# Weight slots of the last stage filled while the second mixer ends, and the first mixer's last sums stored in the second

## The chip, the core and the metric

The kernel runs on one core of one Trainium2 chip. Its time is the device time of one launch in microseconds (us), lower is better. TensorE multiplies matrices and transposes, VectorE (DVE in the rows), ScalarE (ACT) and GpSimd (POOL) work on whole tiles, and SyncE (SP) issues the transfers between the chip's main memory and the on-chip memory. Each engine has its own list of instructions and runs it in order; semaphores hold an engine until another one, or a transfer, has got far enough.

## The reference

One encoder layer on 2048 tokens of width 1024:

```python
xn = rms_norm(h, g_attn_pre)
qa, ka, va, qb, kb, vb = split(xn @ w_in)
ya = mixer_a(qa, ka, va)       # grouped attention over all tokens, 8 query heads, 2 key heads
yb = mixer_b(qb, kb, vb)       # dilated windows with a position bias, 8 heads
y = concat(rms_norm(ya, g_out_a), rms_norm(yb, g_out_b)) @ w_out
h = h + rms_norm(y, g_attn_post)
f = square(relu(rms_norm(h, g_mlp_pre) @ w_ff1)) @ w_ff2
h = h + rms_norm(f, g_mlp_post)
gate = sigmoid(rms_norm(h, g_ple) @ w_ple_gate)
h = h + gate * (p @ w_ple_proj)
```

Everything is float32. Most factors are split into a high and a low part (the names end in `_hi` and `_lo`), and a product is then three matmuls: high by high, high by low, low by high.

## The kernel before

It has four stages, each a block of its own with a program for each engine. At the end of a block all engines meet at a barrier, and what SyncE must have seen land is waited for there. The stages are `project_phase`, `mixer_a_phase`, `mixer_b_phase` and `feed_phase`; in the rows their tiles begin with `proj`, `mixa`, `mixb` and `feed`. Orders are written out by hand in each engine's function; no scheduler is at work. Tiles live in the on-chip memory, some from the left (for one stage) and some from the right (`side="right"`, kept over into the next stage).

**First mixer.** 16 query blocks of 128 rows, two groups of heads each. For each unit VectorE writes two half products into `y_half` (L1089), GpSimd adds the halves (L833) and the parts (L837) into `y_st`, and SyncE stores it (L715). The last such pair of sums, `summed(2 * NT + 1, ...)`, and its store stand at the very end of the block.

**Second mixer.** 8 heads of 16 units; even heads use the first of two sets of keys, queries and values (`kT[0]`, `qT[0]`, `v_hl[0]`), odd heads the second. The last head is odd. GpSimd splits the next head's inputs in units 0 to 7, then copies its bias tables (`other_tables`, `end_tables`), and in each unit adds two halves (L1343) that TensorE transposes back (L1438). It opens the stage with memsets and the first head's tables. SyncE loads the next head's inputs behind waits for these splits: keys (L88), queries (L93), values (L98 and 24 small ones, L106), tables (L113, L119). Before the last head it loads the constants of the next stage, and after that head's first store the rows of `total` (L145, L146).

**Last stage.** It works on blocks of 512 tokens. The first block starts with the output product: for each of four token tiles TensorE transposes (L1872) and multiplies (L1964) 24 times with the weights in four slots `w_split`, 1 MB each, then 24 times with those in `w_far`, four more pieces of 1 MB that lie in `feed_comb` for now. Later all weights go through the four slots (L1881): some are loaded as pairs from `wG`, others are loaded raw and split by ScalarE and GpSimd. SyncE's list at the start of the stage is: four slots (L1757), four residual tiles `res` (L1772), four far pieces (L1775), each waiting for its slot's landing, and four raw weights (L1778).

Of the kernel before, what the change touches and what calls it, by code (L numbers as in the profile page):

```python
# [15 lines left out]
F32 = mybir.dt.float32  # L16
F32R = mybir.dt.float32r
# [3 lines left out]
P = 128  # L21
# [47 lines left out]
class HeadInputs:  # L69
# [6 lines left out]
    def __init__(self, nc, ctx, scr):  # L76
        k = Kit(nc, ctx, "mixb")
        self.scr = scr
        self.q_in = k.sb("q_in", [P, S])
        self.k_in = k.sb("k_in", [P, S])  # L80
        self.v_in = k.sb("v_in", [P, self.VT, HD])
        self.t_near = k.sb("t_near", [P, TABLE_W - OWN_W])
        self.t_own = [k.sb(f"t_own{u}", [P, 7 * P]) for u in range(2)]
        self.k_dma, self.q_dma, self.v_dma, self.t_dma = (k.sem(n) for n in ("k_dma", "q_dma", "v_dma", "t_dma"))

# [37 lines left out]
class FeedInputs:  # L123
# [6 lines left out]
    def __init__(self, nc, ctx):  # L130
        k = Kit(nc, ctx, "feed")
        self.total = k.sb("total", [P, TT, D], side="right")
        self.g_row = k.sb("g_row", [P, 2, D], side="right")
        self.gate_in = k.sb("gate_in", [P, 3, KD], side="right")
        self.const_in = k.sem("const_in")
        self.w_dma, self.out_dma = k.sems("w_dma", self.NR4), k.sems("out_dma", TT)

    def load_consts(self, sp, gates, gains):
        for i, g in enumerate(gates):
            sp.dma_start(self.gate_in[:, i, :], g).then_inc(self.const_in, 16)  # L140
        for i, g in enumerate(gains):
            sp.dma_start(self.g_row[:, i, :], row_broadcast(g)).then_inc(self.const_in, 16)

    def load_y(self, sp, scr, t):
# [493 lines left out]
def mixer_a_phase(nc, scr, step, ident, first, heads, w_ff2, w_late):  # L638
# [12 lines left out]
    with ExitStack() as ctx:  # L651
# [8 lines left out]
        oT = k.sb("oT", [P, 2, BANK])  # L660
        y_half = k.sb("y_half", [P, 2, G * 2 * HD])
        q_raw = heads.t_own[1][:, 0:G * P]
        y_st = k.sb("y_st", [P, 2, G * HD])
        nmax = k.sb("nmax", [P, 2, 2, G])
# [23 lines left out]
        row_done, merge, scale_done = k.sem("row_done"), k.sem("merge"), k.sem("scale_done")  # L688
        o_done, fold_done, half_done, y_done = (k.sem(n) for n in ("o_done", "fold_done", "half_done", "y_done"))
        y_out = k.sems("y_out", 2)  # L690
# [16 lines left out]
        def _(sp):  # L707
# [81 lines left out]
            one(NT - 1, None)  # L789
            store(1, slice(NT * P, NT * P + P), 2 * NT + 1)  # L790
            sp.wait_ge(y_out[0], 16 * (NT + 1))
            sp.wait_ge(y_out[1], 16 * (NT + 2))
            sp.wait_ge(q_dma, 32 * NT)

        @block.gpsimd
        def _(pool):
# [101 lines left out]
            for it in range(NHB + SPLIT_ITS + 1, NT):  # L898
                for w in range(2):
                    unit(it, w)  # L900
            summed(2 * NT + 1, 1, 16 * NT + 16, 2 * NT * MERGE + 1)

# [230 lines left out]
def mixer_b_phase(nc, scr, step, ident, heads, feed, consts):  # L1133
# [13 lines left out]
    with ExitStack() as ctx:  # L1147
        k = Kit(nc, ctx, "mixb")
        q_in, k_in, v_in, t_near, t_own = heads.q_in, heads.k_in, heads.v_in, heads.t_near, heads.t_own
        kT = [[k.sb(f"kT{u}{h}", [P, SW], F32R) for h in range(2)] for u in range(2)]  # L1150
        qT = [k.sb(f"qT{u}", [P, S], F32R) for u in range(2)]
        v_hl = [k.sb(f"v_hl{u}", [P, VT, 2 * HD], F32R) for u in range(2)]
        t_oth = [k.sb(f"t_oth{u}", [P, 6, P]) for u in range(2)]
# [41 lines left out]
        def _(sp):  # L1195
# [34 lines left out]
            sp.wait_ge(pre_lo, len(FIRST_ORDER))  # L1230
            heads.load_k(sp, 1)
            sp.wait_ge(pre_lo, PRE)
            heads.load_q(sp, 1)
            next_v(0, 1)
            next_tables(0, 0, 1)
            for h in range(NHB - 1):
                one(h)
            feed.load_consts(sp, *consts)
            store(NHB - 1, 0)
            sp.wait_ge(y_out[0], 32 * NHB)  # L1240
            sp.wait_ge(y_out[1], 32 * NHB - 16)
            for t in range(TT):
                feed.load_y(sp, scr, t)
# [13 lines left out]
        def _(pool):  # L1257
# [56 lines left out]
            def split_values(h, par, m):  # L1314
# [7 lines left out]
                pool.tensor_tensor(low, v_in[:, at, :], hi.bitcast(F32), ALU.subtract).then_inc(v_lo, 1)  # L1322

            borders(0)
            pool.wait_ge(set_done, 3)
            pool.wait_ge(t_dma, 32)
            other_tables(0)
            end_tables(0, (0,))
            borders(1)
            pool.memset(o_sum[:, 1, :], 0.0).then_inc(set_done, 1)  # L1330
# [278 lines left out]
def feed_phase(nc, x, w_ff2, w_tail, pT_d, scr, out, step, ident, feed):  # L1609
# [44 lines left out]
    with ExitStack() as ctx:  # L1654
# [11 lines left out]
        w_raw = k.sb("w_raw", [P, NR4, CW])  # L1666
        w_sp = [k.sb(f"w_split{i}", [P, 2, CW], F32R) for i in range(NSPL4)]
        res = k.sb("res", [P, TT, D])
# [54 lines left out]
        def _(sp):  # L1723
# [29 lines left out]
            def load_split(C, j, slot):  # L1753

                if not (isinstance(C, int) and C < NSPL4):
                    sp.wait_ge(w_used, C - NSPL4 + 2)
                sp.dma_start(w_sp[slot][:].bitcast(F32), scr["wG"][j]).then_inc(w_dma[slot], 16)  # L1757
# [10 lines left out]

            for C in range(NSPL4):
                load_split(C, C, C)  # L1770
            for t in range(TT):
                sp.dma_start(res[:, t, :], x[t * P:(t + 1) * P, :]).then_inc(x_dma[t], 16)  # L1772
            for q in range(NR4):
                sp.wait_ge(w_dma[q], 16)
                sp.dma_start(w_far[q].bitcast(F32), scr["wG"][NR4 + q]).then_inc(w_dma[q], 16)  # L1775
            for i in range(NR4):
                sp.wait_ge(w_dma[i], 16 * (NG1 // NR4))
# [764 lines left out]
```

## Time and profile before

| | |
|---|---|
| median of 3 runs | 3391.04 us (3388.26 to 3392.82) |
| the profiled execution | 3389.53 us |
| its span | 3387.7 us |
| TensorE busy | 3301.4 us, 97% of the span |
| VectorE busy | 2298.8 us, 68% |
| ScalarE busy | 1857.0 us, 55% |
| GpSimd busy | 1856.9 us, 55% |
| transfers | 503.39 MB, mean 149 GB/s |

The span is from the first to the last instruction of one profiled execution; the time of that execution is a little longer. TensorE's share is the mean over all stages, so what matters for a change is where TensorE isn't busy, and what it waits for there. In the rows, L with a number is a line of the kernel, "SPq" is SyncE's queue of transfers, and "[2.57 <-DVE feed_xT L2266]" means that the engine sat idle for 2.57 us before this row and that VectorE's instruction of line 2266, writing `feed_xT`, ended that. A row may stand for several alike ("x24").

### The profile page before, as it was taken

The numbers are of one execution on the slowest core, as the hardware profiler recorded it, in microseconds if no ns is written. First come the engines' busy times: TensorE is split into PE (matmuls) and PEld (weight loads), VectorE is DVE, ScalarE is ACT, GpSimd is POOL, SyncE is SP. The second block draws the span as 40 slices with busy tenths as digits, with TensorE's granted clock in tenths as the row PEclk, the third lists the DMA queues.
The fourth block names the chain that finished last, engine by engine and source line by source line (L and its number), as shares of the span: only waits on it lengthen the run. The fifth ranks groups of instructions, "written<-read, shape, count | busy, mean of one in ns | idle before, by whom it ended". The sixth has DMA issues, their size and how long they took to land.

```text
span 3387.7 us, 48305 instructions
## 1 busy us (share of the span) xinstructions
PE 3301.4 (97%) x17246; PEld 2772.3 (82%) x17246; DVE 2298.8 (68%) x4080; ACT 1857.0 (55%) x3576; POOL 1856.9 (55%) x1434
## 2 busy tenths in 40 slices
PE   8999999999999989998999999999999999999997
PEld 7888878888888879996888887888888888888886
DVE  6565579999999889996656565565655557455554
ACT  3221178888888879997544453344534445443342
POOL 5555534445452178872477732777417775067770
PEclk9999999999999999998999999999999999999998
DMA  5554434444442134434244466444564444744443
GB/s 190 174 174 151 141 115 137 145 165 155 168 156 67 43 89 107 102 83 175 79 142 149 149 220 225 140 151 148 180 243 155 155 146 160 261 146 143 142 139 133
DMA packets 223915, 503.39 MB, mean 149 GB/s; under 512 B 105428, under 2 KB 123420, under 8 KB 204476
## 3 DMA queue, kind: packets, MB, share of 16 engines
q1 hardware_dynamic: 214332, 486.57, 43.6%
q10 hardware_dynamic: 9344, 13.73, 1.1%
q8 instruction: 138, 2.26, 0.3%
q14 instruction: 101, 0.83, 0.1%
HBM read 417.09 MB, written 95.58 MB: 151 GB/s over the span
## 4 chain that ended last, share of the span: by engine, by line
PE 47%; DVE 2%; DMA 1%; ACT 1%; issue 1%; POOL 0%; SPq 0%; DVEq 0%
PE feed_bank L1881 45%; PE feed_bank L1872 1%; PE feed_bank L1964 1%; PE feed_bank L2016 1%; ACT feed_xT L2110 0%; DMA feed_w_split<-scr_wG 0%; DMA feed_comb<-scr_wG 0%; PE feed_bank L1987 0%; POOL feed_w_split L1838 0%; DMA feed_y_in<-scr_yB 0%; DVE feed_xT L2266 0%; DVE feed_sums L2402 0%; DVE feed_total L2356 0%; ACT feed_w_split L2162 0%; DVE feed_res L2284 0%
## 5 line engine op out<-in xcount | busy, mean ns | idle before, releaser
L1838 POOL TENSOR_TENSOR feed_w_split<-feed_w_raw,feed_w_split 128x1024 fp32r<-128x1024 f32 x352 | 881.7, 2515 | 249.5 <-ACT feed_w_split L2162 236.3
L1881 PE MATMUL feed_bank<-feed_w_split,feed_comb 128*128 128x512 f32 x3552 | 822.2, 391 | 16.6 <-DVE feed_sums L2402 7.8
L1881 PEld LDWEIGHTS feed_bank<-feed_w_split,feed_comb 128*128 128x128 f32 x3552 | 664.4, 188 | 162.7 <-POOL feed_w_split L1838 11.8
L1881 PE MATMUL feed_bank<-feed_xT,feed_w_split 128*128 128x512 f32 x2976 | 677.6, 389 | 0.6 <-ACT feed_rl L2177 0.6
L1881 PEld LDWEIGHTS feed_bank<-feed_xT,feed_w_split 128*128 128x128 f32 x2976 | 558.3, 188 | 117.2 <-issue 1.5
L1115 DVE TENSOR_TENSOR mixa_pT<-mixa_turned,mixa_pT 128x512 fp32r<-128x512 f32 x512 | 350.8, 685 | 58.8 <-ACT mixa_pT L1057 51.6
L1835 POOL TENSOR_SCALAR feed_w_split<-feed_w_raw 128x1024 fp32r<-128x1024 f32 x128 | 138.0, 1078 | 452.1 <-PE feed_bank L1881 193.5
L1057 ACT ACTIVATE mixa_pT<-mixa_turned 128x512 fp32r<-128x512 f32 x512 | 306.6, 599 | 118.6 <-PE mixa_turned L993 99.5
L938 PE MATMUL mixa_out_acc<-mixa_pT,mixa_v_hl 128*128 128x512 f32 x1028 | 365.7, 437 | 0.2
L2356 DVE TENSOR_TENSOR feed_total<-feed_total,feed_bank 128x512 f32<-128x512 f32 x352 | 224.4, 681 | 197.1 <-PE feed_bank L1881 194.2
L2177 ACT ACTIVATE feed_rl<-feed_bank 128x512 f32<-128x512 f32 x128 | 76.4, 597 | 506.5 <-PE feed_bank L1881 499.7
L2162 ACT ACTIVATE feed_w_split<-feed_w_raw 128x1024 fp32r<-128x1024 f32 x224 | 235.8, 1061 | 187.8 <-PE feed_bank L1881 183.4
L1082 DVE TENSOR_REDUCE mixa_nmax<-mixa_score 128x1 f32<-128x1024 f32 x256 | 312.6, 1221 | 8.1 <-PE mixa_score L925 1.3
L993 PE MATMUL mixa_turned<-layer_ident,mixa_prob 128*128 128x128 f32 x2048 | 307.2, 273 | 0.9 <-DVE mixa_pT L1115 0.7
L993 PEld LDWEIGHTS mixa_turned<-layer_ident,mixa_prob 128*128 128x128 f32 x2048 | 251.7, 141 | 59.8 <-DVE mixa_pT L1115 3.7
L1027 ACT ACTIVATE mixa_prob<-mixa_score,mixa_nmax 128x1024 f32<-128x1024 f32 x256 | 286.2, 1118 | 3.2 <-DVE mixa_nmax L1082 3.1
L925 PE MATMUL mixa_score<-mixa_kT,mixa_qT 128*128 128x512 f32 x1024 | 279.4, 394 | 2.9 <-ACT mixa_prob L1027 2.4
L2325 DVE TENSOR_TENSOR feed_comb<-feed_rl,feed_comb 128x256 fp32r<-128x256 f32 x128 | 150.6, 1179 | 164.9 <-ACT feed_comb L2181 164.6
L925 PEld LDWEIGHTS mixa_score<-mixa_kT,mixa_qT 128*128 128x128 f32 x1024 | 191.6, 188 | 49.7 <-ACT mixa_prob L1027 4.1
L436 PE MATMUL proj_bank<-proj_w_split,proj_xT 128*128 128x512 f32 (+1 forms) x752 | 173.2, 354 | 0.0
L365 POOL TENSOR_TENSOR proj_w_split<-proj_w_raw,proj_w_split 128x2048 fp32r<-128x2048 f32 x35 | 163.7, 4676 | 2.9
L362 POOL TENSOR_SCALAR proj_w_split<-proj_w_raw 128x2048 fp32r<-128x2048 f32 x35 | 70.0, 2001 | 163.0 <-issue 162.6
(212 smaller groups left out, 5498.0 us busy)
## 6 DMA issues: line engine op xcount, KB each, us to landing
feed_w_raw<-scr_wT SPq DMA_DIRECT2D x160, 512.0 KB, 3.3
feed_w_split<-scr_wG SPq DMA_DIRECT2D x68, 1024.0 KB, 4.9
feed_w_raw<-w_tail_dram SPq DMA_DIRECT2D x128, 512.0 KB, 3.5
proj_w_raw<-w_in_dram SPq DMA_DIRECT2D x36, 1024.0 KB, 5.6
feed_w_raw<-w_ff_dram SPq DMA_DIRECT2D x64, 512.0 KB, 3.4
scr_table<-scr_bias SPq DMA_DIRECT2D x8, 1520.0 KB, 9.0
scr_wG<-mixb_q_in SPq DMA_DIRECT2D x9, 1024.0 KB, 3.9
scr_wG<-mixb_k_in SPq DMA_DIRECT2D x9, 1024.0 KB, 7.0
```

Source lines behind the costliest of these rows:

```text
L436: mm = pe.matmul(acc[t][:, 0:width], xT[u][a][:, k0 + kk, t * P:(t + 1) * P], w[m][:, kk, :], start=begin, stop=end)
L925: mm = pe.matmul(score[:, at * BANK:(at + 1) * BANK], qT[g][:, h, :], kT[g][part][:, kc * BANK:(kc + 1) * BANK], start=part == 0, stop=par ...
L938: mm = pe.matmul(out_acc[half][:], v_hl[:, s, g, :], pT[part][:, s % NR, :], start=s % (NT // 2) == 0 and part == 0, stop=s % (NT // 2) == ...
L993: mm = pe.transpose(turned[s % 2][:, h * P:(h + 1) * P], prob[w][:, h, s * P:(s + 1) * P], ident[:])
L1027: act.activation(prob[par][:, h, half * 2 * BANK:(half + 1) * 2 * BANK], score[:, 2 * (c % 2) * BANK:2 * (c % 2 + 1) * BANK], ACT.Exp, bia ...
L1057: act.activation(pT[0][:, s % NR, :], turned[s % 2][:], ACT.Copy).then_inc(hi_done, 1)
L1082: ve.tensor_reduce(nmax[:, par, c // G, c % G:c % G + 1], score[:, 2 * (c % 2) * BANK: 2 * (c % 2 + 1) * BANK], AXX, ALU.max, negate=True) ...
L1115: ve.tensor_tensor(pT[1][:, s % NR, :], turned[s % 2][:], pT[0][:, s % NR, :].bitcast(F32), ALU.subtract).then_inc(lo_done, 1)
L1838: pool.tensor_tensor(w_sp[slot][:, 1, :], w_raw[:, slot, :], w_sp[slot][:, 0, :].bitcast(F32), ALU.subtract).then_inc(w_lo, 1)
L1881: mm = pe.matmul(dst, lhs, rhs, start=start, stop=stop)
L2162: act.activation(w_sp[slot][:, 0, :], w_raw[:, slot, :], ACT.Copy).then_inc(w_hi_ff, 1)
L2356: ve.tensor_tensor(at, at, acc[2 * (n % 2) + t][:], ALU.add if sign > 0 else ALU.subtract).then_inc(ev_dve, 1)
```

## The change

There are three edits.

1. The first mixer's last pair of sums leaves its block. GpSimd makes them in the second mixer's opening list (`last_of_first`), SyncE stores them there. The tiles that it needs, `a_half` and `a_st`, move to the class whose tiles live in both mixers.
2. The four weight slots of the last stage are no tiles of their own any more. They are laid over `v_hl[0]`, `qT[0]` and `kT[0][0]`, the even set of the second mixer, which are now allocated from the right. They are loaded in the second mixer once the values of head 6 are used (`pv_done`), in front of the last head's first store. The last stage's list then starts with the far pieces, and the residual tiles come behind these.
3. A tile `line` of 32 bytes is put ahead of them, which with the ones beside it makes the slots start 64 bytes past a multiple of 128 (196416, 204736, 212928 and 221120 in a partition). Before, the slots started at 138240, a multiple of 128, and the following ones 8192 further each. Tiles beside them move by whole multiples of 128 bytes or, for `total`, `g_row` and `gate_in`, by one that isn't.

The diff, with what only renames left out:

```diff
@@ HeadInputs.__init__
+        self.a_half = k.sb("a_half", [P, 2, D_AB])
+        self.a_st = k.sb("a_st", [P, 2, D_AB // 2])
+        self.a_half_done, self.a_summed, self.a_out = (k.sem(n) for n in ("a_half_done", "a_summed", "a_out"))
@@ FeedInputs
+        k.sb("line", [P, 8], side="right")
+        self.v_hl = k.sb("v_hl0", [P, HeadInputs.VT, 2 * HD], F32R, side="right")
+        self.qT = k.sb("qT0", [P, S], F32R, side="right")
+        self.kT = k.sb("kT0", [P, S + 2 * PAD], F32R, side="right")
+        self.w_sp = [a.rearrange("p (h c) -> p h c", h=2) for a in
+                     (self.v_hl[:, 0:16, :].rearrange("p n c -> p (n c)"),
+                      self.v_hl[:, 16:32, :].rearrange("p n c -> p (n c)"), self.qT[:], self.kT[:, 0:2 * self.CW])]
...
+    def load_first(self, sp, scr, C):
+        sp.dma_start(self.w_sp[C].bitcast(F32), scr["wG"][C]).then_inc(self.w_dma[C], 16)
@@ mixer_a_phase, SyncE
             one(NT - 1, None)
-            store(1, slice(NT * P, NT * P + P), 2 * NT + 1)
             sp.wait_ge(y_out[0], 16 * (NT + 1))
-            sp.wait_ge(y_out[1], 16 * (NT + 2))
+            sp.wait_ge(y_out[1], 16 * (NT + 1))
@@ mixer_a_phase, GpSimd
                 for w in range(2):
                     unit(it, w)
-            summed(2 * NT + 1, 1, 16 * NT + 16, 2 * NT * MERGE + 1)
@@ mixer_b_phase, SyncE
             heads.load_k(sp, 1)
+            sp.wait_ge(heads.a_summed, 2)
+            sp.dma_start(scr["yA"][S:S + P, D_AB // 2:D_AB], heads.a_st[:, 1, :]).then_inc(heads.a_out, 16)
             sp.wait_ge(pre_lo, PRE)
...
             feed.load_consts(sp, *consts)
+            sp.wait_ge(pv_done, (NHB - 1) * NU)
+            for C in range(NSPL4):
+                feed.load_first(sp, scr, C)
             store(NHB - 1, 0)
             sp.wait_ge(y_out[0], 32 * NHB)
             sp.wait_ge(y_out[1], 32 * NHB - 16)
+            sp.wait_ge(heads.a_out, 16)
@@ mixer_b_phase, GpSimd
+            def last_of_first():
+                both, parts = heads.a_half, heads.a_half[:, 0, :].rearrange("p (h a d) -> p h a d", a=2, d=HD)
+                pool.wait_ge(heads.a_half_done, 4 * NU + 2)
+                pool.tensor_tensor(both[:, 0, :], both[:, 0, :], both[:, 1, :], ALU.add).then_inc(heads.a_summed, 1)
+                pool.wait_ge(heads.a_summed, 1)
+                pool.tensor_tensor(heads.a_st[:, 1, :].rearrange("p (h d) -> p h d", d=HD), parts[:, :, 0, :],
+                                   parts[:, :, 1, :], ALU.add).then_inc(heads.a_summed, 1)
...
             end_tables(0, (0,))
+            last_of_first()
             borders(1)
@@ feed_phase, SyncE
-            for C in range(NSPL4):
-                load_split(C, C, C)
-            for t in range(TT):
-                sp.dma_start(res[:, t, :], x[t * P:(t + 1) * P, :]).then_inc(x_dma[t], 16)
             for q in range(NR4):
                 sp.wait_ge(w_dma[q], 16)
                 sp.dma_start(w_far[q].bitcast(F32), scr["wG"][NR4 + q]).then_inc(w_dma[q], 16)
+            for t in range(TT):
+                sp.dma_start(res[:, t, :], x[t * P:(t + 1) * P, :]).then_inc(x_dma[t], 16)
```

SyncE's list at the start of the last stage, before:

```order
L1757 DMA feed_w_split<-scr_wG 128x2048 x4
L1772 DMA feed_res<-x_dram 128x1024 x4
L1775 DMA feed_comb<-scr_wG 128x2048 [waits feed_w_dma0]
L1775 DMA feed_comb<-scr_wG 128x2048 [waits feed_w_dma1]
L1775 DMA feed_comb<-scr_wG 128x2048 [waits feed_w_dma2]
L1775 DMA feed_comb<-scr_wG 128x2048 [waits feed_w_dma3]
L1778 DMA feed_w_raw<-w_tail_dram 128x1024 [waits feed_w_dma0]
```

And of the changed kernel, whose line numbers are its own:

```order
L1797 DMA feed_comb<-scr_wG 128x2048 [waits feed_w_dma0]
L1797 DMA feed_comb<-scr_wG 128x2048 [waits feed_w_dma1]
L1797 DMA feed_comb<-scr_wG 128x2048 [waits feed_w_dma2]
L1797 DMA feed_comb<-scr_wG 128x2048 [waits feed_w_dma3]
L1799 DMA feed_res<-x_dram 128x1024 x4
L1802 DMA feed_w_raw<-w_tail_dram 128x1024 [waits feed_w_dma0]
```

The slot loads are gone from the list, and the far pieces stand ahead of the residual tiles. The slot loads now stand in SyncE's list of the second mixer, in front of the last head's first store; under the names of the tiles they lie over:

```order
L152 DMA feed_g_row<-g_attn_post_dram 128x1024
L152 DMA feed_g_row<-g_mlp_post_dram 128x1024
L155 DMA feed_v_hl<-scr_wG 128x2048 [waits mixb_pv_done]
L155 DMA feed_v_hl<-scr_wG 128x2048
L155 DMA feed_qT<-scr_wG 128x2048
L155 DMA feed_kT<-scr_wG 128x2048
L1225 DMA scr_yB<-mixb_y_st 128x4x64 [waits mixb_y_ready]
L158 DMA feed_total<-scr_yA 128x512 [waits mixb_a_out,mixb_y_out1,mixb_y_out0]
```

Before, that store followed right on the two `feed_g_row` loads. GpSimd's opening list of the second mixer, from the first head's tables on, before:

```order
L1275 COPY mixb_t_oth<-mixb_t_near 128x384
L1289 COPY mixb_t_end<-mixb_t_near 128x96
L1290 COPY mixb_t_end<-mixb_t_near 128x3x16
L1292 COPY mixb_t_end<-mixb_t_near 128x3x16
L1260 MEMSET mixb_kT 128x16
L1261 MEMSET mixb_kT 128x16
```

And of the changed kernel:

```order
L1292 COPY mixb_t_oth<-mixb_t_near 128x384
L1306 COPY mixb_t_end<-mixb_t_near 128x96
L1307 COPY mixb_t_end<-mixb_t_near 128x3x16
L1309 COPY mixb_t_end<-mixb_t_near 128x3x16
L1345 TENSOR_TENSOR mixb_a_half<-mixb_a_half 128x512 [waits mixb_a_half_done]
L1347 TENSOR_TENSOR mixb_a_st<-mixb_a_half 128x256 [waits mixb_a_summed]
L1277 MEMSET mixb_kT 128x16
L1278 MEMSET mixb_kT 128x16
```

The two additions have moved in between the first tables and the memsets.

## Rows read from the trace of the kernel before

**Rows 1.** Table of stages: stretch, length, then busy time (instructions) of each engine.

```profile
1582.00:1680.00 98.00, 85.44 (x472) 73.28 (x472) 53.74 (x115) 45.09 (x127) 31.06 (x16) 0.92 0.43 167
```

**Rows 2.** The chain that ended last: start, us, what is on it.

```profile
1583.39 11.21 DMA feed_w_split<-scr_wG
1594.63 15.66 DMA feed_comb<-scr_wG
1610.33 1.66 PE feed_bank L1964 x6
...
3350.66 4.71 DMA feed_w_split<-scr_wG
```

**Rows 3.** Timeline of the last stage's start: start, us, engine, what [idle before].

```profile
1582.07 2.00 SPq L1757 DMA_DIRECT2D feed_w_split<-scr_wG  x4
...
1590.44 7.82 PE L1964 MATMUL feed_bank<-feed_w_split,feed_xT 128*128 128x512 f32 x24 [2.57 <-DVE feed_xT L2266]
...
1594.63 0.32 SPq L1775 DMA_DIRECT2D feed_comb<-scr_wG  x1
...
1598.10 1.03 PE L1872 MATMUL feed_bank<-layer_ident,feed_xn 128*128 128x128 f32 x8
...
1611.83 1.03 PE L1872 MATMUL feed_bank<-layer_ident,feed_xn 128*128 128x128 f32 x8
...
1617.69 1.23 DVE L2284 TENSOR_TENSOR feed_res<-feed_res,feed_total 128x1024 f32<-128x1024 f32 x1
...
1618.17 1.04 PE L1872 MATMUL feed_bank<-layer_ident,feed_xn 128*128 128x128 f32 x8
```

**Rows 4.** Timeline where the two mixers meet.

```profile
1193.06 0.69 DVE L1089 TENSOR_TENSOR mixa_y_half<-mixa_out_acc,mixa_factor 128x512 f32<-128x512 f32 x1 [2.17 <-PE mixa_out_acc L947]
1193.83 1.26 POOL L833 TENSOR_TENSOR mixa_y_half<-mixa_y_half 128x512 f32<-128x512 f32 x1 [10.87 <-DVE mixa_y_half L1089]
1195.17 0.72 POOL L837 TENSOR_TENSOR mixa_y_st<-mixa_y_half 128x256 f32<-128x256 f32 x1
1195.91 0.32 SPq L715 DMA_DIRECT2D scr_yA<-mixa_y_st  x1
...
1198.13 0.63 ACT L1471 ACTIVATE mixb_kT<-mixb_k_in 128x512 fp32r<-128x512 f32 x1 [5.82 <-PEq L651]
```

**Rows 5.** Waits of SyncE's queue from 1195 to 1262: total, times, longest.

```profile
SPq L793 <- DMA scr_yA<-mixa_y_st: 1.4, 1, 1.4
```

**Rows 6.** Timeline of the second mixer's first head.

```profile
1207.95 1.27 DVE L1541 TENSOR_TENSOR mixb_v_hl<-mixb_v_in,mixb_v_hl 128x1024 fp32r<-128x1024 f32 x1
1208.01 1.29 POOL L1290 COPY mixb_t_end<-mixb_t_near 128x48 f32<-128x48 f32 x1
...
1209.25 0.22 POOL L1292 COPY mixb_t_end<-mixb_t_near 128x48 f32<-128x48 f32 x1
...
1215.82 1.08 SPq L93 DMA_DIRECT2D mixb_q_in<-scr_qBT  x2
...
1235.88 0.56 SPq L119 DMA_DIRECT2D mixb_t_own<-scr_table  x1
...
1241.35 0.95 POOL L1275 COPY mixb_t_oth<-mixb_t_near 128x384 f32<-128x384 f32 x2 [1.65 <-DMA mixb_t_own<-scr_table]
...
1243.73 0.33 PE L1438 MATMUL mixb_out_acc<-layer_ident,mixb_o_sum 128*128 128x128 f32 x1 [0.48 <-POOL mixb_o_sum L1343]
```

**Rows 7.** Groups by line and shape: busy us, mean ns | idle before.

```profile
L433 PE MATMUL proj_bank<-proj_xT,proj_w_split 128*128 128x512 f32 x512 | 138.4, 390 | 0.0
L433 PE MATMUL proj_bank<-mixa_keys,proj_w_split 128*128 128x512 f32 x256 | 80.8, 392 | 0.0
L1881 PE MATMUL feed_bank<-feed_w_split,feed_comb 128*128 128x512 f32 x3552 | 822.2, 391 | 16.6 <-DVE feed_sums L2402 7.8 <-issue 4.2 <-DVE feed_comb L2383 1.9
L1881 PE MATMUL feed_bank<-feed_xT,feed_w_split 128*128 128x512 f32 x2976 | 677.6, 389 | 0.6 <-ACT feed_rl L2177 0.6
L1881 PE MATMUL feed_bank<-feed_w_split,feed_xT 128*128 128x512 f32 x576 | 134.3, 391 | 0.0
```

**Rows 8.** Instructions on `feed_total` from 1570 to 1660: ns min/median/max.

```profile
L2101 ACT ACTIVATE feed_junk<-feed_total x8: 612/616/677, 1582.1 to 1591.6; 128x512 bf16<-128x512 f32 x8
```

More of the change, by code:

```diff
@@ L660, in mixer_a_phase @@
         oT = k.sb("oT", [P, 2, BANK])
-        y_half = k.sb("y_half", [P, 2, G * 2 * HD])
+        y_half = heads.a_half
         q_raw = heads.t_own[1][:, 0:G * P]
-        y_st = k.sb("y_st", [P, 2, G * HD])
+        y_st = heads.a_st
         nmax = k.sb("nmax", [P, 2, 2, G])
@@ L688, in mixer_a_phase @@
         row_done, merge, scale_done = k.sem("row_done"), k.sem("merge"), k.sem("scale_done")
-        o_done, fold_done, half_done, y_done = (k.sem(n) for n in ("o_done", "fold_done", "half_done", "y_done"))
+        o_done, fold_done, half_done, y_done = k.sem("o_done"), k.sem("fold_done"), heads.a_half_done, k.sem("y_done")
         y_out = k.sems("y_out", 2)
@@ L1149, in mixer_b_phase @@
         q_in, k_in, v_in, t_near, t_own = heads.q_in, heads.k_in, heads.v_in, heads.t_near, heads.t_own
-        kT = [[k.sb(f"kT{u}{h}", [P, SW], F32R) for h in range(2)] for u in range(2)]
-        qT = [k.sb(f"qT{u}", [P, S], F32R) for u in range(2)]
-        v_hl = [k.sb(f"v_hl{u}", [P, VT, 2 * HD], F32R) for u in range(2)]
+        kT = [[feed.kT, k.sb("kT01", [P, SW], F32R)], [k.sb(f"kT1{h}", [P, SW], F32R) for h in range(2)]]
+        qT = [feed.qT, k.sb("qT1", [P, S], F32R)]
+        v_hl = [feed.v_hl, k.sb("v_hl1", [P, VT, 2 * HD], F32R)]
         t_oth = [k.sb(f"t_oth{u}", [P, 6, P]) for u in range(2)]
@@ L1666, in feed_phase @@
         w_raw = k.sb("w_raw", [P, NR4, CW])
-        w_sp = [k.sb(f"w_split{i}", [P, 2, CW], F32R) for i in range(NSPL4)]
+        w_sp = feed.w_sp
         res = k.sb("res", [P, TT, D])
@@ L1753, in load_split @@
             def load_split(C, j, slot):
-                if not (isinstance(C, int) and C < NSPL4):
-                    sp.wait_ge(w_used, C - NSPL4 + 2)
+                sp.wait_ge(w_used, C - NSPL4 + 2)
                 sp.dma_start(w_sp[slot][:].bitcast(F32), scr["wG"][j]).then_inc(w_dma[slot], 16)
```

## The prediction

> **What bounds the kernel now.** I read the stage table first, then the chain of waits, then the timeline where two stages meet. TensorE works through nearly the whole span; the exception this change can reach is the start of the last stage, where the row for 1582 to 1680 us shows 85.44 us of work in 98 [rows 1]. The chain of waits says why: it begins there with two transfers, 11.21 us for the four weight slots and 15.66 us for the four far slots (`feed_comb`), and TensorE is on it from 1610.33 only [rows 2].
>
> The timeline gives the detail [rows 3]. SyncE issues the four slot loads from 1582.07. The far loads wait for the slots one by one; the last is issued at 1594.63, when the fourth slot has landed. TensorE starts the first output half (24 matmuls, token tile 0) at 1590.44 when VectorE has finished the transposed input, not when a slot lands: it runs 7.82 us with no stall. After 8 transposes at 1598.10 comes the other half, on the far slots, which waits for `feed_comb` until 1610.33, so that the next transposes come at 1611.83. The same pair later, with nothing missing, goes from 1611.83 to 1618.17: 6.34 us.
>
> The other meeting point is that of the two mixers [rows 4]. VectorE's last product ends at 1193.75 (1193.06 + 0.69). Then GpSimd adds twice (1.26 and 0.72 us), SyncE issues a store that takes 0.32 from 1195.91, and waits 1.4 us for its landing [rows 5]. The engines start again at 1198.13, 0.5 us after that landing at about 1197.6.
>
> **The change part by part.** *Slots filled in the second mixer's last head.* The four loads leave the start of the last stage, so SyncE issues the far loads where the slots were. Four transfers of 1 MB from 1582.07 had landed by 1594.63 [rows 3]; the far ones are as large and take that place, 12.6 us. TensorE reaches them after the transposes of 1598.10, with 4 us to spare. It then runs on at the undisturbed pace, and the next transposes start at 1598.10 + 6.34 = 1604.44 instead of 1611.83: 7.4 us gained. That is the bound from above too, since everything ahead of 1598.10 stays as it is. From below: if the far loads landed 3 us later than the slots did, past 1598.9, 2 us of it would be lost. The residual tiles now follow the far ones: 2 MB more at the same rate, until about 1601. VectorE first uses one at 1617.69 [rows 3], now about 1610.3, so they are hidden by 9 us. The raw weights come behind them, by about 1607 (2 MB more); GpSimd first splits one when the last token tile's matmuls free a slot, and three tiles still come after 1604. So the rest of the stage shifts as it stands.
>
> In the last head the four loads queue on SyncE ahead of the first store of that head and of the loads of `total`. The four megabytes need 12.6 us; a head has (1582.07 - 1198.13)/8 = 48 us [rows 3, 4]. The store and the loads of `total` may land later by that much at worst, and `total` is first read in the next stage. Nothing on the path; I take 0. The upper end is 1.2 us: in a stretch of full transfer load one ScalarE row took 677 ns where 612 is its minimum [rows 8], 65/612 = 11% more; 12.6 us x 0.11 = 1.3 at the most, 1.2 since ScalarE isn't busy all of it.
>
> *First mixer's last sums.* The barrier no longer waits for GpSimd, the store and its landing. With the same 0.5 us from the last event to the restart it opens at 1193.75 + 0.5 = 1194.25 instead of 1198.13: 3.9 us gained.
>
> The two additions now stand in GpSimd's opening list, ahead of eight memsets and twelve copies of the end tables. From 1193.83 to 1195.89 they took 2.06 us; with the wait between them 2.1. Is GpSimd covered there? After the copies it splits the queries; SyncE then issues the next queries at 1215.82, behind them 25 loads of values, and the second of the two tables at 1235.88. GpSimd waits 1.65 us for these tables at 1241.35, and TensorE waits 0.48 us for GpSimd at 1243.73 [rows 6]. So this chain, from the GpSimd list through SyncE's queue to TensorE, ends last at unit 8 of the first head: 2.1 us more in the list is 2.1 us more at TensorE, though the units before may hide part of it. Later heads do not win it back, as TensorE has hardly any idle time there. I charge 2.1. From below 0 (all hidden), from above 3.2: one more stall of the kind that the copy at 1208.01 shows, 1.29 us beside a VectorE product of 1.27 us begun at 1207.95, against 0.22 for the copy of the same shape behind it, so 1.1 us.
>
> That row is where a rule bears on the price. The Trainium skill (SBUF — State Buffer, "Who interferes with whom") says that a VectorE instruction with two SBUF inputs and a GpSimd one that reads SBUF exclude each other, and that a GpSimd write alone does not clash. The trace agrees, with 1.29 us against 0.22. By the rule, if the moved additions bring the memsets wholly beside VectorE's product, that stall of 1.1 us would vanish and the gain be 10.3; by the rows as they stand it stays, and the gain is 9.2.
>
> *New places in memory.* The slots, and the even set of keys, queries and values, start 64 bytes past a multiple of 128; the slots had started on one. No row shows exactly that. The nearest: in the projection the same matmul with stationary rows from `mixa_keys`, 96 bytes past a multiple of 128, takes 392 ns, from `proj_xT` on a multiple 390 [rows 7]. I take 0 for it, and keep +2 ns a matmul (and -2, as nothing rules out the reverse, though such a mean mixes clocks) as the ends.
>
> One rule speaks against this part. The Trainium skill (DMA: Bandwidth & Descriptors, "How a descriptor splits into AXI transactions") says that a piece not starting at a multiple of 256 bytes costs one transaction more: 33 for 32 in rows of 8 KB, 3%. No run here shows it for the slots. Only one slot load stands in the open in the chain, 4.71 us near the end [rows 2], so the gain by it would be 9.05 instead of 9.2.
>
> **The sum.** -7.4 - 3.9 + 2.1 = -9.2 us. The profiled execution took 3389.53 (span 3387.7), so 3380.3 by its own time. The median of the runs is 1.5 us above that execution: 3391.04 - 9.2 = 3381.8.
>
> **Rivals.**
> (A) GpSimd's two additions are hidden: for it speaks that it waits 1.65 us for the tables anyway; against it, that these tables depend on GpSimd's own splits. -7.4 - 3.9 = -11.3: 3379.7.
> (B) The slot loads disturb the last head by 1.2 us: -8.0, 3383.0. Against it, only one row in eight shows that slowdown.
> (C) The hand-over between the mixers doesn't do what it says: the additions cost as much in the second mixer as they did before the barrier, 3.9 us, through a stall on top and the tables' queue. What is left is the last stage's gain, -7.4: 3383.6. For it speaks that the list goes through two further queues before TensorE sees it.
> (D) Slower: the slots' new place costs TensorE. It reads a slot in 3552 + 2976 + 576 = 7104 matmuls [rows 7]. At 2 ns each that is 14.2 us, against 9.2 gained: +5.0, 3396.0. It decides from 1.3 ns a matmul. Against it, the 2 ns are a difference of means of two groups that ran at different moments, and a mean takes in the stretches at the lower clock.
>
> **How the numbers follow.** Forecast 0.60 (own range 3380 to 3383.7), A 0.13, B 0.09, C 0.12, D 0.06. The range of 8 in 10 goes from 3378.2, below A by the spread of the runs, to 3386.0, above C by 2.4 us: the far loads landing late or a GpSimd cost of 3.2 with B. It leaves out D. A change under 0.2%, 6.8 us, can't be told from none. Faster means under 3384.3: nearly all of the forecast and A, most of B and C, 0.82. No change: the rest of these, 0.12. Slower: D, 0.06.
>
> **What would show it.** In the profile of the changed kernel: the first `feed_comb` load is issued at the stage's start, TensorE has no wait for `feed_comb`, and the second transposes follow the first by about 6.3 us; the chain no longer begins with `feed_w_split`. Between the mixers the first ScalarE row comes 0.5 us after VectorE's last product; the first wait for the tables at GpSimd, counted from the second mixer's start, comes 2.1 us later (A: TensorE's unit 8 comes no later; C: later by nearly 4). B would show in ScalarE rows of the last head, D in a step from transposes to transposes of the last stage that is no longer 6.34 us. Wrong would be the whole if SyncE still waits at the last stage's start for something that takes the slots' place, or if the head-7 store is late enough to hold the barrier.

## The result: slower, and where the time went

| | before | changed |
|---|---|---|
| median | 3389.81 us (5 runs, beside the changed one) | 3407.64 us (5 runs, 3406.09 to 3410.65) |
| ratio, 95% interval | | 1.0054 [1.0042, 1.0066] |
| span of the profiled execution | 3387.7 us | 3405.9 us |
| TensorE busy | 3301.4 us | 3330.9 us |

17.8 us slower, where 9.2 faster was forecast. I cut the two spans at the second mixer's first ScalarE instruction and at the last stage's first transposes:

| stretch | before | changed | difference |
|---|---|---|---|
| up to the second mixer | 1198.13 | 1194.58 | -3.55 |
| second mixer | 387.77 | 388.30 | +0.5 |
| last stage | 1801.8 | 1823.0 | +21.2 |

The three edits first, since their gains are there. The stage table, in the columns of [rows 1], for the 98 us from the last stage's start:

```profile
1579.00:1677.00 98.00, 89.65 (x500) 77.07 (x500) 60.24 (x125) 50.36 (x135) 32.32 (x16) 0.93 0.35 129
```

TensorE does 500 matmuls and transposes where it did 472. The chain of waits no longer begins with two transfers [rows 2]; it is TensorE from 1587.42 on:

```profile
1587.42 7.91 PE feed_bank L1988 x24
1595.33 0.87 PE feed_bank L1896 x8
1596.20 5.50 PE feed_bank L1988 x24
1601.71 0.87 PE feed_bank L1896 x8
1602.58 5.58 PE feed_bank L1988 x24
```

The timeline there [rows 3]:

```profile
1579.05 1.92 SPq L1797 DMA_DIRECT2D feed_comb<-scr_wG  x4
...
1595.17 1.04 PE L1896 MATMUL feed_bank<-layer_ident,feed_xn 128*128 128x128 f32 x8
...
1601.54 1.04 PE L1896 MATMUL feed_bank<-layer_ident,feed_xn 128*128 128x128 f32 x8
...
1607.42 1.23 DVE L2308 TENSOR_TENSOR feed_res<-feed_res,feed_total 128x1024 f32<-128x1024 f32 x1
```

The far loads are the first that SyncE issues, and the second transposes come 6.37 us behind the first, as forecast (6.34), where it was 13.73. (The next step, whose 24 matmuls read the slots, already shows the loss: 6.46 us to the transposes of 1608.00, where it was 6.34.) Where the mixers meet [rows 4]:

```profile
1193.53 0.69 DVE L1100 TENSOR_TENSOR mixb_a_half<-mixa_out_acc,mixa_factor 128x512 f32<-128x512 f32 x1 [2.17 <-PE mixa_out_acc L958]
...
1194.58 0.63 ACT L1498 ACTIVATE feed_kT<-mixb_k_in 128x512 fp32r<-128x512 f32 x1 [1.79 <-PEq L664]
```

From VectorE's last product to ScalarE's first row it is 0.36 us (1194.58 less 1193.53 + 0.69), where it was 4.38: 4.0 gained, 3.9 forecast. And the first head [rows 6]:

```profile
1200.43 1.27 POOL L1345 TENSOR_TENSOR mixb_a_half<-mixb_a_half 128x512 f32<-128x512 f32 x1
...
1204.52 1.27 POOL L1306 COPY mixb_t_end<-mixb_t_near 128x32 f32<-128x32 f32 x1
...
1214.33 1.09 SPq L96 DMA_DIRECT2D mixb_q_in<-scr_qBT  x2
...
1238.13 0.96 POOL L1292 COPY mixb_t_oth<-mixb_t_near 128x384 f32<-128x384 f32 x2 [0.66 <-DMA mixb_t_own<-scr_table]
...
1240.79 0.27 PE L1465 MATMUL mixb_out_acc<-layer_ident,mixb_o_sum 128*128 128x128 f32 x1
```

Counted from the mixer's first ScalarE row, the query load comes 19.75 us in, where it was 17.69: the 2.1 us of the two additions, as charged. But the tables reach GpSimd at 43.55 against 43.22, and TensorE's unit 8 comes at 46.2 against 45.6. Only 0.6 of the 2.1 is left by then: the 24 value loads behind the queries took SyncE's queue 16.65 us, where they had taken 17.78, and the tables behind them reached GpSimd sooner after their issue.

So the kernel stood some 10 us ahead at 1601.54 (1611.83 before). Then it lost it. The groups by line and shape, in the columns of [rows 7]:

```profile
L1905 PE MATMUL feed_bank<-feed_v_hl,feed_comb 128*128 128x512 f32 x1776 | 428.1, 396 | 6.4 <-DVE feed_sums L2426 4.8 <-issue 1.3 <-POOL feed_v_hl L1862 0.2
L1905 PE MATMUL feed_bank<-feed_xT,feed_v_hl 128*128 128x512 f32 x1488 | 347.6, 393 | 0.9 <-ACT feed_rl L2201 0.9
L1905 PE MATMUL feed_bank<-feed_kT,feed_comb 128*128 128x512 f32 x888 | 215.4, 393 | 3.8 <-DVE feed_sums L2426 2.6 <-DMA feed_kT<-scr_wG 0.9 <-POOL feed_kT L1862 0.3
L1905 PE MATMUL feed_bank<-feed_xT,feed_kT 128*128 128x512 f32 x744 | 178.6, 395 | 0.0
```

A matmul has a stationary operand, 128 columns that a weight load puts into TensorE, and a moving one, here 512 columns, that it is multiplied with. In such a row the tile named first moves and the second is stationary: the kernel gives `comb[:, a, n, 2 * pair + kk, t * P:(t + 1) * P]`, 128 columns, as the stationary operand and 512 columns of the slot as the moving one, and the row says `feed_v_hl,feed_comb`. The prediction and the expectations below take the two roles the other way round. They compare the same pairs of tiles, so what they forecast for a row stands once "stationary" and "moving" are exchanged in them; in this text they are as the kernel has them.

Every group that reads a slot has grown, from 389 to 391 ns before to 392 to 397, and by different amounts: the first two slots (`v_hl`) cost more as the moving operand, the last (`kT`) more as the stationary one. The mean length of a matmul isn't its cost in a stream, since neighbours overlap. That is the time from one start to the next, which I took from the starts in the trace (means over those under 300 ns, without the waits):

| operands | before | changed |
|---|---|---|
| slot moving, `comb` stationary | 227.1 | v_hl 233.1, qT 233.3, kT 229.3 |
| `xT` moving, slot stationary | 226.7 | v_hl 230.1, qT 229.3, kT 233.2 |
| slot moving, `xT` stationary | 227.2 | v_hl 233.3, qT 233.3, kT 229.0 |

Counts times differences come to 32.7 us over the 7104 matmuls of this line, 4.6 ns each. Nothing else in the stage has grown like it: a slot load takes 4.8 to 5.1 us where it took 4.9, and weight loads to the array last 188 ns in both.

### The profile page after: what moved, and what is told of

Its sections match the earlier page's. It is cut to its first block, busy times and chain, and to the rows that moved or that the text cites. A ratio compares the mean times of both kernels' runs of the same rounds, so it can differ in the third digit from the quotient of the medians.

```text
span 3405.9 us, 48304 instructions
## 1 busy us (share of the span) xinstructions
PE 3330.9 (98%) x17246; PEld 2770.4 (81%) x17246; DVE 2302.6 (68%) x4080; ACT 1859.0 (55%) x3576; POOL 1869.0 (55%) x1434
## 3 DMA queue, kind: packets, MB, share of 16 engines
q10 hardware_dynamic: 9344, 13.73, 1.1%
## 4 chain that ended last, share of the span: by engine, by line
PE 48%; DVE 2%; ACT 1%; issue 1%; DMA 0%; POOL 0%; SPq 0%; DVEq 0%
PE feed_bank L1905 45%; PE feed_bank L1988 1%; PE feed_bank L1896 1%; PE feed_bank L2040 1%; ACT feed_xT L2134 1%; DVE feed_xT L2290 0%; DMA feed_y_in<-scr_yB 0%; PE feed_bank L2011 0%; POOL feed_kT L1862 0%; DVE feed_sums L2426 0%; DVE feed_total L2380 0%; DVE feed_xn L2281 0%; DVE feed_res L2308 0%; DVE feed_ms L2269 0%; ACT feed_junk L2125 0%
## 5 line engine op out<-in xcount | busy, mean ns | idle before, releaser
L1862 POOL TENSOR_TENSOR feed_v_hl<-feed_w_raw,feed_v_hl 128x1024 fp32r<-128x1024 f32 x176 | 448.2, 2553 | 128.1 <-ACT feed_v_hl L2186 122.1
L1905 PE MATMUL feed_bank<-feed_v_hl,feed_comb 128*128 128x512 f32 x1776 | 428.1, 396 | 6.4 <-DVE feed_sums L2426 4.8
L1905 PEld LDWEIGHTS feed_bank<-feed_v_hl,feed_comb 128*128 128x128 f32 x1776 | 331.8, 188 | 88.8 <-DVE feed_sums L2426 6.6
L1905 PE MATMUL feed_bank<-feed_xT,feed_v_hl 128*128 128x512 f32 x1488 | 347.6, 393 | 0.9 <-ACT feed_rl L2201 0.9
L1905 PEld LDWEIGHTS feed_bank<-feed_xT,feed_v_hl 128*128 128x128 f32 x1488 | 279.7, 188 | 63.9 <-issue 1.5
L1862 POOL TENSOR_TENSOR feed_qT<-feed_w_raw,feed_qT 128x1024 fp32r<-128x1024 f32 x88 | 223.1, 2535 | 84.2 <-ACT feed_qT L2186 81.3
L1862 POOL TENSOR_TENSOR feed_kT<-feed_w_raw,feed_kT 128x1024 fp32r<-128x1024 f32 x88 | 223.7, 2542 | 44.0 <-ACT feed_kT L2186 41.2
L1905 PE MATMUL feed_bank<-feed_qT,feed_comb 128*128 128x512 f32 x888 | 218.8, 397 | 3.0 <-DVE feed_comb L2407 1.9
L1905 PE MATMUL feed_bank<-feed_kT,feed_comb 128*128 128x512 f32 x888 | 215.4, 393 | 3.8 <-DVE feed_sums L2426 2.6
L1905 PEld LDWEIGHTS feed_bank<-feed_qT,feed_comb 128*128 128x128 f32 x888 | 165.9, 188 | 45.4 <-POOL feed_kT L1862 3.9
```

Of the source, the lines that this page charges most:

```text
L1862: pool.tensor_tensor(w_sp[slot][:, 1, :], w_raw[:, slot, :], w_sp[slot][:, 0, :].bitcast(F32), ALU.subtract).then_inc(w_lo, 1)
L1905: mm = pe.matmul(dst, lhs, rhs, start=start, stop=stop)
```

## The experiments

Three theories. S: the start address of a slot by itself (off some multiple it is dear). R: the part of memory, or the neighbours (the first expectation calls the neighbours T). O, formed after the first four runs: the offset between the two operands of a matmul. "Modulo 256" means what is left of a number when whole multiples of 256 are taken off. "Start to start" is read as above in each trace; a slot's matmuls were told apart by tile name, or by the order of the weight pieces.

**A filler tile of 96 bytes.**

```diff
-        k.sb("line", [P, 8], side="right")
+        k.sb("line", [P, 24], side="right")
```

> The changed kernel with one size altered: the filler tile ahead of the slots has 96 bytes in place of 32, so all slots start on a multiple of 128 bytes, 64 bytes lower, in the same part of memory. Theory S (the start address): the matmuls of the last stage that read a slot come again every 226.9 ns as before (now 229 to 233 from start to start), the 28 us that the last stage lost are back, and the three gains stay (10.2 us by the trace at 1608): 3389.8 - 10.2 = 3379.6. Theory R (the region: the slots above 196,000 bytes stand in the way of the other operand or of a writer): the pace stays at 229 to 233 ns and the time at 3407 to 3408. Theory T (the slots' loads, splits and stores have become dearer by their new neighbours): the same as R.

Measured: 3407.42 (5 runs), before 3389.01, ratio 1.0053 [1.0041, 1.0066]. Nothing came back, so a multiple of 128 isn't enough. Three slots now start 128 past a multiple of 256 and run at 232.4 to 233.0 ns in either role; `kT`, on one, at 228.1 to 228.7.

**Only the slots of the kernel before, 64 bytes further.**

```diff
+        k.sb("pad0", [P, 16])
         w_sp = [k.sb(f"w_split{i}", [P, 2, CW], F32R) for i in range(NSPL4)]
+        k.sb("pad1", [P, 16])
```

> The kernel before with nothing but a filler tile of 64 bytes ahead of the four slots and one behind them: the slots start at odd multiples of 64 bytes, in their old part of memory. Theory S: the pace of the matmuls on slots goes from 226.9 to 229 to 233 ns and the kernel becomes slower by about 28 us: 3418. Theories R and T: nothing changes, 3389 to 3391.

Measured: 3415.24 (5 runs), ratio 1.0078 [1.0064, 1.0092]: 26 us from two empty tiles. The address alone does it, with the slots in their old part of memory and none of the three edits made. Groups of that kernel:

```profile
L1883 PE MATMUL feed_bank<-feed_w_split,feed_comb 128*128 128x512 f32 x3552 | 828.4, 393 | 14.5 <-DVE feed_sums L2404 7.6 <-issue 2.6 <-DVE feed_comb L2385 1.9
L1883 PE MATMUL feed_bank<-feed_xT,feed_w_split 128*128 128x512 f32 x2976 | 697.2, 395 | 0.9 <-ACT feed_rl L2179 0.9
```

At 64 past, a moving slot runs at 229.3 ns and a stationary one at 233.3. That is `kT` in the changed kernel (196416 = 64 past a multiple of 256); its `v_hl` and `qT` stand 192 past and show the reverse. Shifts of 64 and 192 mirror each other, as a difference taken the one way or the other does.

**No filler tile: slots 96 past a multiple of 128.**

```diff
-        k.sb("line", [P, 8], side="right")
```

> The changed kernel without the filler tile: the slots start 96 bytes past a multiple of 128. Theory S in its plain form (whatever is off the multiple pays): as the changed kernel, 3407 to 3408, or more, since it is off the 64 too. Theory S, narrow form (only odd multiples of 64 pay): the projection's stationary operand of the kernel before stood 96 bytes past and kept 226.9 ns, so 3379.6. Theory R: 3407 to 3408.

Measured: 3419.07 (4 runs), ratio 1.0092 [1.0078, 1.0105], all groups at 233.2 to 233.9 ns. The narrow form of S falls, and so does my use of the projection's rows: its tile stood equally far off and kept 227. A reason is in the list of addresses: the projection's split weights (128224, 144608) and that tile (212960) are all 224 past a multiple of 256. Their difference is 0. That is theory O, which the next runs put to the test.

**The first mixer's sums alone**, on the kernel before: `store(1, ...)` and `summed(...)` leave the first mixer, `last_of_first` and its store stand in the second.

> The kernel before with one part of the change: the first mixer's last sums are stored in the second mixer. By my steps: -3.9 at the hand-over and +2.1 for the two additions in the opening list, 1.8 gained, 3388.0. By the trace of the changed kernel, in which TensorE's first instruction of the second mixer comes 3.6 us earlier and its unit 8 comes 2.9 us earlier: 3386.9. Rival: the additions cost as much there as they gave, 3389.8.

Measured: 3386.50 (11 runs), before 3389.01, ratio 0.9993 [0.9984, 1.0002]: 2.5 us by the medians, which the interval does not tell from none. In its trace the hand-over takes 0.36 us and the second mixer 388.8.

**Everything in the last stage's left part shifted by 64, distances kept.**

```diff
+        k.sb("pad", [P, 16])
         xT = [k.sb(f"xT{h}", [P, KD, BT], F32R) for h in range(2)]
```

> The kernel before with a filler tile of 64 bytes ahead of the transposed input, so that this, the product buffer, the raw weights and the slots all start 64 bytes past a multiple of 128 and of 256, with the same distances between them as before. Theory O (what counts is the offset between the two operands of a matmul, the slot's start against that of the other operand, modulo 256 bytes): nothing changes, 226.9 ns from start to start and 3389 to 3391. Theory S (the start of each tile by itself, on a multiple of 256): at least the loss of the kernel with only the slots shifted, +26 us: 3415 or more.

Measured: 3388.61 (11 runs), ratio 0.9998 [0.9989, 1.0007]; 227.0, 226.7 and 227.0 ns:

```profile
L1882 PE MATMUL feed_bank<-feed_w_split,feed_comb 128*128 128x512 f32 x3552 | 820.2, 390 | 16.9 <-DVE feed_sums L2403 7.8 <-POOL feed_w_split L1839 4.1 <-issue 2.0
L1882 PE MATMUL feed_bank<-feed_xT,feed_w_split 128*128 128x512 f32 x2976 | 677.5, 389 | 0.6 <-ACT feed_rl L2178 0.6
```

S falls: every tile is off, and nothing is lost. This and the kernel with only the slots shifted have their slots at the same addresses and differ by 26.6 us.

**The other operands moved to meet three of the slots**, in the changed kernel.

```diff
+        k.sb("pad", [P, 48])
         xT = [k.sb(f"xT{h}", [P, KD, BT], F32R) for h in range(2)]
```

> The changed kernel with a filler tile of 192 bytes ahead of the transposed input: this and the product buffer now start 192 bytes past a multiple of 256, as the slots of v_hl and qT do, while the slot of kT, at 64, is 128 off. Theory O: pairs with v_hl and qT go back to 227 ns, pairs with kT go to about 232.8 ns (from 229.3 and 233.2). The three good slots win back 1776 and 888 matmuls of 6.1 ns, 1488 and 744 of 2.6 to 3.3, 432 of 6.3: about 25 us; kT's lose 888+144 x 3.6 = 3.7: 3407.6 - 21 = 3386 to 3387. Theory S: nothing is won, 3407 or more.

Measured: 3390.45 (10 runs), ratio 1.0002 [0.9993, 1.0011]. The slots haven't moved, and 17 us are back, some 4 fewer than O's sum of 21, which took the products in full (on that, see the next kernel). The groups split as O says:

```profile
L1906 PE MATMUL feed_bank<-feed_xT,feed_v_hl 128*128 128x512 f32 x1488 | 343.0, 389 | 0.6 <-ACT feed_rl L2202 0.6
L1906 PE MATMUL feed_bank<-feed_xT,feed_kT 128*128 128x512 f32 x744 | 178.3, 395 | 0.0
L1906 PE MATMUL feed_bank<-feed_xT,feed_qT 128*128 128x512 f32 x744 | 173.9, 389 | 0.0
L1906 PE MATMUL feed_bank<-feed_kT,feed_xT 128*128 128x512 f32 x144 | 34.7, 396 | 0.0
L1906 PE MATMUL feed_bank<-feed_qT,feed_xT 128*128 128x512 f32 x144 | 33.9, 391 | 0.0
```

**The change with all slots on multiples of 256**, and once with 120 columns for 56, which moves the first three to multiples of 512.

```diff
-        k.sb("line", [P, 8], side="right")
+        k.sb("line", [P, 56], side="right")
...
+        k.sb("gap", [P, 32], side="right")
         self.kT = k.sb("kT0", [P, S + 2 * PAD], F32R, side="right")
```

> The changed kernel with the filler tile at 224 bytes in place of 32 and a gap of 128 bytes between the slots of kT and qT, so that all four slots start on a multiple of 256 (v_hl and qT 256 past a multiple of 512, kT on one), as the input and the product buffer do. Theory O, modulo 256: all pairs at 226.9 ns, the 28 us are back and the gains of the change stay: 3379.6. Theory S: the same. If the modulus is 512: v_hl and qT stay slow, kT is fast: about 3398 to 3402. Theory R (the region): 3407.

> As the kernel with all slots on multiples of 256, but the filler tile has 480 bytes: v_hl and qT start on multiples of 512, kT 256 past one. Theories O and S, modulo 256: 3379.6, the same as that kernel. If the modulus is 512: v_hl and qT fast, only kT's 1776 matmuls slow by up to 6 ns: 3380 to 3390. Theory R: 3407.

Measured: 3378.86 for both (6 runs each), ratio 0.9970 [0.9958, 0.9981] and [0.9959, 0.9982], every group at 226.7 to 227.3 ns. Faster than both kernels, before and changed; R falls, and the modulus is not 512. Groups of the first:

```profile
L1906 PE MATMUL feed_bank<-feed_v_hl,feed_comb 128*128 128x512 f32 x1776 | 417.5, 391 | 7.7 <-DVE feed_sums L2427 5.2 <-POOL feed_v_hl L1863 1.9 <-issue 0.6
L1906 PE MATMUL feed_bank<-feed_xT,feed_v_hl 128*128 128x512 f32 x1488 | 342.7, 389 | 0.6 <-ACT feed_rl L2202 0.6
L1906 PE MATMUL feed_bank<-feed_kT,feed_comb 128*128 128x512 f32 x888 | 213.4, 390 | 4.8 <-DVE feed_sums L2427 2.6 <-POOL feed_kT L1863 1.2 <-DMA feed_kT<-scr_wG 1.0
L1906 PE MATMUL feed_bank<-feed_xT,feed_kT 128*128 128x512 f32 x744 | 173.7, 389 | 0.0
```

Its last stage takes 1793.7 us, 29.3 less than the changed kernel's. The products gave 32.7; some is taken up by waits, for TensorE idles 17.4 us ahead of these matmuls in this kernel (7.7, 4.8, 4.3 ahead of `qT` with `comb`, 0.6) and 14.1 in the changed one (6.4, 3.8, 3.0, 0.9).

**A map of offsets**: the kernel before with its slots 32, 96, 160 and 224 past a multiple of 256.

```diff
-        w_sp = [k.sb(f"w_split{i}", [P, 2, CW], F32R) for i in range(NSPL4)]
+        w_sp = []
+        for name, ahead in zip(("at32_", "at96_", "at160_", "at224_"), (8, 16, 16, 16)):
+            k.sb("pad_" + name, [P, ahead])
+            w_sp.append(k.sb(name + "s", [P, 2, CW], F32R))
+        k.sb("pad_last", [P, 8])
```

> The kernel before with filler tiles, so that its four slots start 32, 96, 160 and 224 bytes past a multiple of 256, the input and the product buffer on one: one look for the pace of each offset in both roles. Theory O with a price that hangs on the offset alone (stationary start less moving start, modulo 256), whichever role the slot has: a stationary slot at 96 gives what a moving slot at 160 gives and the other way round (both near 233.3 ns by the kernel without filler), a stationary slot at 32 what a moving one at 224 gives, a stationary one at 224 what a moving one at 32 gives; all between 227 and 234, and the whole 3411 to 3417. Rival: each role has its own price, and the mirrored pairs differ by over 1 ns.

Measured: 3431.26 in one run, span 3429.5, 41.8 us over that of before; the sum had been put too low (7104 matmuls at 6.4 ns are 45). With the kernels above it fills the map, in ns from start to start:

| moving start less stationary start, modulo 256 | 0 | 32 | 64 | 96 | 128 | 160 | 192 | 224 |
|---|---|---|---|---|---|---|---|---|
| slot moving | 227.2 | 233.3 | 229.2 | 233.6 | 232.9 | 233.6 | 233.2 | 233.4 |
| slot stationary | 226.8 | 233.5 | 229.8 | 233.4 | 232.6 | 234.1 | 233.3 | 233.1 |

The starts stand for all pieces, since in these tiles every piece that a matmul reads begins a multiple of 512 bytes past its tile's start. The two roles agree within 0.6 ns at every offset: the price hangs on the difference and not on the role. The values at 32, 96, 160 and 224 rest on this one run; the kernel with no filler tile has each of these four differences in one of the roles, at 233.2 to 233.9.

**The other edits alone, slots on multiples of 256.**

> The other part of the change alone, with the slots on multiples of 256: they are filled in the second mixer's last head, the far ones at the last stage's start, and the first mixer's last sums are stored before the barrier as in the kernel before. By my step for the last stage's start: 7.4 gained, 3389.3 - 7.4 = 3381.9. Rival B (the slots' loads disturb the last head): 1.2 less, 3383.1. If moving the residual tiles behind the far ones or the wait for them cost something: 3384 or more.

Measured: 3382.48 (11 runs), before 3388.93, ratio 0.9979 [0.9970, 0.9987]: 6.5 us, 7.4 forecast and inside the interval. The second mixer takes 387.8 us with the slots' loads in its last head, as it did without them (387.77), so rival B's 1.2 us are not there. The new places of the mixer's own even set cost nothing there either.

**The two additions a head later**, with slots on multiples of 256.

```diff
-            last_of_first()
...
                     halves(h * NU + n, n)
+                    if h == 0 and n == NU - 1:
+                        last_of_first()
```

(The store's move in SyncE's list is left out here.)

> The change with slots on multiples of 256, and GpSimd's two additions of the first mixer's sums at the end of the second mixer's first head, their store behind that head's stores in SyncE's queue. By my charge of 2.1 us for the additions in the opening list: 3378.9 - 2.1 = 3376.8. By the trace of the changed kernel, where 0.6 us is what is left of it at the last stage's start (3.55 us ahead at the second mixer's start, 3.0 at the last stage's): 3378.3. Rival: the additions disturb the head they are moved to as much, 3378.9.

Measured: 3378.79 (7 runs), the same as at the list's start. The second mixer takes 388.5 us, where it took 389.0 (additions in the opening list) and 387.8 (none). 3376.8 is out; what the place of the additions is worth is too little for these times.

**Another stage.** The tile of the projection, 64 bytes lower.

```diff
+        k.sb("pad", [P, 16], side="right")
         self.xT = k.sb("keys", [P, KD, BT], F32R, side="right")
```

> The kernel before with a filler tile of 64 bytes above the tile that holds a quarter of the projection's transposed input: this tile starts 160 past a multiple of 256, where it stood at 224, and the projection's split weights stay at 224. Another stage, other tiles. Theory O: where that tile is stationary (256 matmuls of 512 columns) its start less that of the weights is 192 modulo 256, and the pace goes from 227.1 ns to about 233.3; where it is moving (224 of 512 columns) the difference is 64, and the pace goes from 226.9 to about 229.4. The other projection matmuls and the last stage stay at 227. In time some 2 us, too little for one look. Theory S: the tile was off a multiple of 256 before and is so now, so nothing changes, 227.1 and 226.9.

Measured: 3391.21 in one run, 3388.60 for before beside it, too little to rest on. The groups, against 392 and 391 before:

```profile
L434 PE MATMUL proj_bank<-mixa_keys,proj_w_split 128*128 128x512 f32 x256 | 82.2, 397 | 0.0
L437 PE MATMUL proj_bank<-proj_w_split,mixa_keys 128*128 128x512 f32 x224 | 70.1, 395 | 0.0
```

From start to start 232.8 and 230.3 ns, where it was 227.1 and 226.9. O's forecasts for the two groups (233.3 and 229.4) hold in a stage that the change doesn't touch; in truth the tile moves in the first row and is stationary in the second. One thing O doesn't give: `xT` moving over the weights, whose own difference stayed 0, went to 237.4 ns where it stands between two matmuls of the shifted tile, while the 372 that stand among their like kept 227.0. Such a set of three takes 703 ns, where it took 681. The delay reaches over to a neighbour.

## Why the prediction was wrong

**The step that failed** is "New places in memory", "I take 0 for it, and keep +2 ns a matmul". It measured 4.6 ns on average over the 7104 matmuls and 29.3 us in the stage. The mechanism stood there as rival D, at 0.06, with its deciding point at 1.3 ns, and with half the size. Two faults. I read the price of a start address from the projection's `mixa_keys` against its `proj_xT`, "on a multiple", and that is wrong: the three tiles called `proj_xT` start at 54496, 70880 and 87264, 96 past a multiple of 128 like `mixa_keys`, and their partner, the split weights, stands there as well. Both rows are one case, with a difference of 0 between the operands and 227.1 ns from start to start, so their 392 and 390 say nothing of a shift. (`mixa_keys` is also the moving operand there, not the stationary one.) And the bound of 2 ns came from these rows too, which could not show the effect: where no row shows a price that is paid 7104 times, and 1.3 ns of it turns the sign, 0.06 was too little.

**The last stage's start**, -7.4: right, 7.36 by the transposes (13.73 less 6.37), 6.5 by time.

**The hand-over**, -3.9: right, 4.0 in the trace.

**The additions**, +2.1: right at GpSimd's split and too high at the end. In the seven kernels that have them in the opening list the second mixer takes 388.3 to 389.8 us, 0.5 to 2.0 more than the 387.8 of the kernels without, 1.0 in the median. The step that was missed is that the queue of transfers behind the delay runs faster: its 24 value loads take 15.8 to 17.3 us in those seven kernels and 17.6 to 18.2 in the seven others; why they do stays open. The stall beside VectorE's value product is still there, only on another copy (1.27 us at 1204.52), so the rule's outcome of 10.3 didn't come about.

**Slot loads in the last head**, 0: right. As to their start off a multiple of 256, a slot load takes 4.8 to 5.1 us in the changed kernel and 4.8 to 5.0 with the slots on multiples of 256, so the 3% that the prediction names is neither shown nor excluded.

**The sum without the slots' price**, -9.2: the kernel with aligned slots is 10.1 to 10.4 us faster than before (3388.93 and 3389.25 less 3378.86), which is -7.4 - 3.9 + 1.0. The changed kernel is slower than this one by 28.8 us (3407.64 less 3378.86), which is TensorE's pace in the last stage (29.3 us between the two traces), and that turns the gain into +17.8, within 0.6 us, by which the medians of before differ.

The Trainium skill (TensorE: Matmul & The Clock Gate, "Step-by-step: what each phase is for") says that TensorE reads its two operands through ports of their own, and that loading the next weights doesn't steal read bandwidth from a running matmul. By that alone the places of the two operands would not matter to each other. Here they do: with both at a difference of 0 the pace is 227 ns, and at 32 it is 233.3. Whether it is the load of the next weights that meets the stream, or something else in the reading, no run here shows, so the sentence on the ports is neither confirmed nor refuted; the traces tell starts of matmuls, and the delay reaches over to later ones.

## What to carry to other kernels

Where TensorE sets the pace with 512-column float32 matmuls whose weights change each time, start the tiles of both operands at the same place modulo 256 bytes. A wrong offset cost 26 to 42 us here, and in the changed kernel a filler tile of 224 bytes and a gap of 128 won 28.8 back. When a change moves tiles, list the new start addresses in pairs, operand with operand, before anything else is priced. And a row that shows no effect bounds it only if the effect could have shown in it.

## What the hardware did that I had not expected

Besides the map above: the price isn't monotonous, since a difference of 64 costs 2 to 3 ns and all the other multiples of 32 up to 224 cost 5.7 to 7.3. Matmuls of 256 columns go the other way. Those of L1987, `xT` moving and slot stationary, come every 119.8 ns at a difference of 0, 117.8 at 64, 118.6 at 128 and 115.5 at 192. So an offset made TensorE faster there, by 1 to 4 ns, but only 192 of them stand on that line; 128 such matmuls of the projection agree, with 121.2 ns at 0 and 117.8 at 64.

Where one slot was at 0 and the three others at 128 (the filler of 96 bytes), the one at 0 ran at 228.1 to 228.7 ns and not at 227. The trace shows where: its matmuls with `xT` come in rows of 24 right behind delayed matmuls on another slot. The first nine of a row come every 231.2 ns on average, the next fourteen every 226.6 to 226.7. So a delay is carried over into matmuls whose own difference is 0, as in the projection, and dies out; what carries it stays open.
